# Sums over channels and heads: products of the full array in place of GpSimd sums and column tiles

## What is computed

```python
def layer(x, ...):
    h = rms_norm(x, norm_mix)
    p = h @ w_in
    y_a, ... = rwkv7_mix(p[..., :SHIFT_COLS], ...)      # 8 heads x 64
    y_b, ... = conv_mix(p[..., SHIFT_COLS:], ...)       # 512 channels
    x = x + concatenate([y_a, y_b], axis=-1) @ w_out
    x = x + moe_ffn(rms_norm(x, norm_ffn), ...)         # top 4 of 32 experts

# at the end of rwkv7_mix: a norm for each token and head, over 64 values
    mu = mean(y, axis=-1); var = mean(square(y - mu), axis=-1)
    y = ((y - mu) * rsqrt(var + GN_EPS)) * lnx_w + lnx_b
    y = (y + bonus) * g

# at the end of conv_mix: a norm for each token, over 512 channels
    mu = mean(z); var = mean(square(z - mu))
    z = (z - mu) * rsqrt(var + LN_EPS) * conv_ln_w + conv_ln_b
    z = z * sigmoid(z)
```

## Time and profile before

| | us |
|---|---|
| median of 3 runs | 1235.98 (1235.7 to 1237.92) |
| the profiled execution, own time | 1235.7 |
| its span | 1233.9 |
| TensorE busy | 1190.7 (96%) |
| VectorE busy | 452.6 (37%) |
| ScalarE busy | 194.5 (16%) |
| GpSimd busy | 73.0 (6%) |
| HBM read | 424.93 MB |

### The profile page before, as it was taken

How to read it: one execution, slowest core, us unless ns; L and a number is a source line. 1 busy time by engine, 2 the same in 40 slices (tenths; PEclk the granted TensorE clock), 3 DMA queues, 4 the chain that set the end, 5 groups by cost and what they waited for, 6 DMA issues and landing times.

```text
span 1233.9 us, 19174 instructions
## 1 busy us (share of the span) xinstructions
PE 1190.7 (96%) x8039; PEld 540.6 (44%) x8039; DVE 452.6 (37%) x987; ACT 194.5 (16%) x387; POOL 73.0 (6%) x113
## 2 busy tenths in 40 slices
PE   7999998999999999999999999999999999999995
PEld 5667798864333333333333333333333333333332
DVE  6657764243522333322222223323222222222324
ACT  3352223224100001101001000010000010000102
POOL 0303433030000000000000000000000000000000
PEclk9999999999999999999999999999999999999998
DMA  9421003188999999999999999999999999999994
GB/s 271 164 69 47 10 5 138 43 325 316 420 420 422 429 428 427 427 428 429 429 428 429 428 429 429 428 429 429 429 428 429 429 428 429 428 429 426 428 429 165
DMA packets 54637, 430.26 MB, mean 349 GB/s; under 512 B 13215, under 2 KB 26959, under 8 KB 29742
## 3 DMA queue, kind: packets, MB, share of 16 engines
q1 hardware_dynamic: 53146, 429.30, 84.1%
q10 hardware_dynamic: 1436, 0.16, 0.1%
HBM read 424.93 MB, written 4.48 MB: 348 GB/s over the span
## 4 chain that ended last, share of the span: by engine, by line
PE 59%; DMA 19%; DVE 1%; ACT 0%; issue 0%; DVEq 0%
PE bank L1793 40%; DMA ring<-in_w_up_dram 19%; PE bank L1771 6%; PE bank L1847 5%; PE bank L1778 2%; PE bank L1673 2%; PE bank L1722 1%; PE bank L1801 1%; PE bank L1819 1%; DVE arena L2138 0%; DVE arena L2132 0%; DVE arena L2078 0%; ACT ring L1619 0%; PE bank L1693 0%; PE bank L1842 0%
## 5 line engine op out<-in xcount | busy, mean ns | idle before, releaser
L1793 PE MATMUL bank<-ring,arena 128*64 128x512 f32 x1536 | 342.2, 594 | 7.2 <-DMA ring<-in_w_up_dram 6.5
L1793 PE MATMUL bank<-arena 128*64 128x512 f32 x1536 | 342.5, 593 | 6.4 <-DMA arena<-in_w_up_dram 6.4
L1793 PEld LDWEIGHTS bank<-ring,arena 128*64 128x64 f32 x1536 | 109.2, 137 | 218.5 <-issue 200.5
L1793 PEld LDWEIGHTS bank<-arena 128*64 128x64 f32 x1536 | 109.0, 136 | 217.2 <-issue 199.4
L2064 DVE TENSOR_SCALAR arena<-bank 128x512 f32<-128x512 f32 x32 | 22.1, 691 | 380.4 <-PE bank L1801 380.4
L2078 DVE TENSOR_TENSOR arena<-arena,bank 128x512 f32<-128x512 f32 x186 | 113.7, 679 | 1.6 <-PE bank L1847 1.6
L524 PE MATMUL bank<-arena,ring 128*128 128x336 f32 x352 | 103.6, 452 | 1.2 <-DVE arena L660 1.2
L1847 PE MATMUL bank<-arena 64*128 64x512 f32 (+1 forms) x384 | 91.1, 606 | 0.7 <-issue 0.7
L1771 PE MATMUL bank<-arena 128*64 128x512 f32 (+1 forms) x384 | 89.5, 600 | 0.1
L2068 DVE TENSOR_SCALAR arena<-bank 128x512 f32<-128x512 f32 x32 | 22.1, 691 | 176.4 <-PE bank L1801 176.4
L524 PEld LDWEIGHTS bank<-arena,ring 128*128 128x128 f32 x352 | 67.1, 192 | 34.8 <-issue 3.3
(11 more groups left out here) (356 smaller groups left out, 821.0 us busy)
## 6 DMA issues: line engine op xcount, KB each, us to landing
ring<-in_w_gate_dram SPq DMA_DIRECT2D x32, 2048.0 KB, 24.8
arena<-in_w_up_dram SPq DMA_DIRECT2D x32, 2048.0 KB, 27.9
ring<-in_w_down_dram SPq DMA_DIRECT2D x32, 2048.0 KB, 31.3
arena<-in_w_gate_dram SPq DMA_DIRECT2D x32, 2048.0 KB, 26.6
ring<-in_w_up_dram SPq DMA_DIRECT2D x32, 2048.0 KB, 29.1
arena<-in_w_down_dram SPq DMA_DIRECT2D x31, 2048.0 KB, 31.0
ring<-in_w_in_dram SPq DMA_DIRECT2D x11, 1024.0 KB, 5.8
ring<-in_w_out_dram SPq DMA_DIRECT2D x4, 1024.0 KB, 8.7
```

The lines of the kernel that those rows point to most:

```text
L1793: mm = M.matmul(bank[64 * hb:64 * hb + 64, b, :], tokens(cc), w[:, c, 512 * hb:512 * hb + 512], start=(cc == 0), stop=(w3 == 2 and cc == K ...
```

## The change

The constant `spread` and its five instructions go. In stage two GpSimd's four sums go; TensorE makes four products that add up in the bank, one for each tile, for the mean and for the variance. In stage three the mean is one product of the full array for each tile with `headones` (sum and spreading at once). The variance is summed onto 8 partitions, one for each head, with a new constant `headcol`, and spread again from these 8 with `headrow`; both are made at the head of stage three from two iotas of GpSimd and three instructions of VectorE. The sums of the variance stand behind d = 1 instead of 2, the rows behind d = 3 instead of 4, and ScalarE's squares stand ahead of its first `take_z`.

```diff
--- before.py
+++ after.py
@@ -117,7 +117,6 @@
         ident = take(P)
         ones = take(P)
         headones = take(P)
-        spread = take(P)
         identc = take(C)
         seqrow = take(NSEQ)
         rowf = take(1)
@@ -699,11 +698,6 @@
                 link(V.tensor_tensor(itmp, itmp, cgrp, ALU.is_equal))
                 V.tensor_tensor(cmask[:, 2, :], cmask[:, 2, :], itmp, ALU.mult)
                 link(V.tensor_tensor(cmask[:, 3, :], cmask[:, 3, :], itmp, ALU.mult))
-                V.tensor_scalar(cgrp, icol, 6, None, ALU.logical_shift_right)
-                link(V.tensor_scalar(itmp, irow, 4, None, ALU.logical_shift_right))
-                link(V.tensor_scalar(itmp, itmp, 1, None, ALU.bitwise_and))
-                link(V.tensor_tensor(itmp, itmp, cgrp, ALU.is_equal))
-                V.tensor_scalar(spread, itmp, 1.0 / 16, None, ALU.mult)
                 dve.wait_ge(R["vec_ready"], 1)
                 link(V.tensor_scalar(vecA[:, V_OMKA:V_OMKA + 4], vecA[:, V_KA:V_KA + 4], -1.0, 1.0,
                                      ALU.mult, ALU.add))
@@ -841,7 +835,7 @@
             return RKq[64 * i:64 * i + 64, :, j * NT + ts:j * NT + ts + n]
 
         names = ["conv_step", "v_turned", "vtok_ready", "hat_ready",
-                 "zmean_done", "z_paired", "z_summed", "z_centered", "z_squared", "zvar_done", "zvar_ready", "zroot_ready", "zinv_ready",
+                 "zmean_done", "z_centered", "z_squared", "zvar_done", "zvar_ready", "zroot_ready", "zinv_ready",
                  "z_normed", "z_affine", "z_sig", "zT_ready",
                  "kt_turned", "bt_turned", "ktok_ready", "btok_ready", "sk_done", "sb_done", "n_done",
                  "sk_read", "sb_read", "n_read", "a0_ready", "n_ready", "at0_ready",
@@ -912,15 +906,8 @@
                     pool.wait_ge(S["n_ready"], p + 1)
                     T.tensor_tensor(AT[p].rearrange("p q j c -> p (q j) c"), n8, b2(cneg0T, 8), ALU.mult)\
                         .then_inc(S["at0_ready"], 1)
+                pool.wait_ge(S["seq4_ready"], 1)
                 pool.wait_ge(S["conv_step"], CONV_LATE)
-                T.tensor_tensor(zsq[:, 0:2, :], zT[:, 0:2, :], zT[:, 2:4, :], ALU.add).then_inc(S["z_paired"], 1)
-                pool.wait_ge(S["z_paired"], 1)
-                T.tensor_tensor(zsq[:, 0, :], zsq[:, 0, :], zsq[:, 1, :], ALU.add).then_inc(S["z_summed"], 1)
-                pool.wait_ge(S["z_squared"], 4)
-                T.tensor_tensor(zsq[:, 0:2, :], zsq[:, 0:2, :], zsq[:, 2:4, :], ALU.add).then_inc(S["z_paired"], 1)
-                pool.wait_ge(S["z_paired"], 2)
-                T.tensor_tensor(zsq[:, 0, :], zsq[:, 0, :], zsq[:, 1, :], ALU.add).then_inc(S["z_summed"], 1)
-                pool.wait_ge(S["seq4_ready"], 1)
                 pool.wait_ge(S["ktok_ready"], 3)
                 pool.wait_ge(S["btok_ready"], 3)
                 s4 = seq4.unsqueeze(1).unsqueeze(3).broadcast_to([P, NPAIR, 4, HD])
@@ -1072,14 +1059,16 @@
                     for p in range(NP3):
                         level_a(l, p)
                     if l == 2:
+                        pe.wait_ge(S["conv_step"], CONV_LATE)
                         pe.wait_ge(S["at_ready"], number_t[(2, 2)] + 1)
-                        pe.wait_ge(S["z_summed"], 1)
-                        M.matmul(bank[:, 7, 0:NT], ones, zsq[:, 0, :], start=True, stop=True)\
-                            .then_inc(S["zmean_done"], 1)
+                        for j in range(4):
+                            mm = M.matmul(bank[:, 7, 0:NT], ones, zT[:, j, :], start=(j == 0), stop=(j == 3))
+                        mm.then_inc(S["zmean_done"], 1)
                     if l == 3:
-                        pe.wait_ge(S["z_summed"], 2)
-                        M.matmul(bank[:, 7, 0:NT], ones, zsq[:, 0, :], start=True, stop=True)\
-                            .then_inc(S["zvar_done"], 1)
+                        pe.wait_ge(S["z_squared"], 4)
+                        for j in range(4):
+                            mm = M.matmul(bank[:, 7, 0:NT], ones, zsq[:, j, :], start=(j == 0), stop=(j == 3))
+                        mm.then_inc(S["zvar_done"], 1)
 
                 level_g(4, 0)
                 level_g(4, 1)
@@ -1327,6 +1316,8 @@
         u1 = at_word(30336, 512)
         sg = at_word(30848, 512)
         sel3 = at_word(29824, 3 * NOVER, NE)
+        headrow = at_word(29824, 512)
+        headrow_i = at_word(30336, 512).bitcast(I32)
         lg4 = at_word(30336, NT)
         sq4 = at_word(30848, NT)
         ycg = at_word(31184, 4, NT)
@@ -1336,6 +1327,9 @@
         Pm = at_word(32528, 3, C)
         esel = at_word(32720, C, dt=BF16)
         rk = at_word(32752, 3)
+        headcol_i = at_word(32756, 4 * NH).bitcast(I32)
+        headcol = at_word(32788, 4, NH)
+        headtmp = at_word(32820, 4 * NH)
         over = [7424]
 
         def bit(*shape, dt=F32):
@@ -1361,7 +1355,8 @@
 
         F = {n: lsem("f_" + n) for n in [
             "x_in", "bias_raw", "wr_in", "gffn_in", "gfin_in", "bias_in",
-            "ysum_done", "ysum_ready", "ymean_done", "y_centered", "y_squared", "yvar_done", "yroot_ready", "yinv_ready", "ybc_done",
+            "headrow_made", "headcol_made", "heads_ready",
+            "ymean_done", "y_centered", "y_squared", "yvar_done", "yroot_ready", "yinv_ready", "ybc_done",
             "yT_ready", "dstep",
             "zp_done", "zp_ready", "zx_ready", "xy_done", "x2_ready", "xsq_ready", "ssq_done", "lg_done", "lg4_ready", "sq4_ready",
             "acc_turned", "acc_ready", "ms_ready", "rms_ready", "wrg_ready", "ssum_done", "logits_done",
@@ -1502,6 +1497,11 @@
             def _(pool):
                 T = nc.gpsimd
 
+                T.iota(headrow_i[0:NH, :].rearrange("p (h k) -> p h k", k=HD), [[1, NH], [0, HD]], base=0,
+                       channel_multiplier=-1).then_inc(F["headrow_made"], 1)
+                T.iota(headcol_i.rearrange("p (j h) -> p j h", h=NH), [[-P, 4], [HD, NH]], base=0,
+                       channel_multiplier=-1).then_inc(F["headcol_made"], 1)
+
                 pool.wait_ge(F["x_in"], 16)
                 for d in range(KC):
                     pool.wait_ge(F["zp_ready"], d + 1)
@@ -1520,24 +1520,21 @@
                 A = nc.scalar
                 act.wait_ge(F["zp_turned"], 1)
                 A.copy(zpT, bank[:, 3, 0:NPAIR * HD].rearrange("p (j k) -> p j k", j=NPAIR)).then_inc(F["zp_copied"], 1)
-                act.wait_ge(F["ysum_done"], 1)
-                A.copy(yrstd, bank[:, 4, 0:NT]).then_inc(F["ysum_ready"], 1)
+                for j in range(4):
+                    act.wait_ge(F["y_centered"], j + 1)
+                    A.activation(ysq[:, j, :], yT[:, j, :], ACT.Square).then_inc(F["y_squared"], 1)
 
                 def take_z(d):
                     act.wait_ge(F["zp_done"], d + 1)
                     A.copy(x2T[:, d, :], bank[:, d % 2, 0:NT]).then_inc(F["zp_ready"], 1)
 
                 take_z(0)
-                for j in range(4):
-                    act.wait_ge(F["y_centered"], j + 1)
-                    A.activation(ysq[:, j, :], yT[:, j, :], ACT.Square).then_inc(F["y_squared"], 1)
                 take_z(1)
-                take_z(2)
                 act.wait_ge(F["yvar_done"], 1)
-                act.wait_ge(F["eps_set"], 1)
-                A.activation(yrstd, bank[:, 2, 0:NT], ACT.Sqrt, bias=eps, scale=1.0 / HD)\
+                act.wait_ge(F["heads_ready"], 1)
+                A.activation(yrstd[0:NH, :], bank[0:NH, 2, 0:NT], ACT.Sqrt, bias=eps[0:NH, :], scale=1.0 / HD)\
                     .then_inc(F["yroot_ready"], 1)
-                for d in range(3, KC):
+                for d in range(2, KC):
                     take_z(d)
 
                 def take_acc(hb, i):
@@ -1647,21 +1644,9 @@
                         mm = M.matmul(bank[64 * i:64 * i + 64, 3, HD * j:HD * j + HD], Zc[64 * i:64 * i + 64, j, :],
                                       ident[64 * i:64 * i + 64, 64 * i:64 * i + 64], start=True, stop=True)
                 mm.then_inc(F["zp_turned"], 1)
-
-                def head_sums(b, v):
-
-                    for j in range(4):
-                        mm = M.matmul(bank[32 * j:32 * j + 32, b, 0:NT], headones[:, 48:80], v[:, j, :],
-                                      start=True, stop=True)
-                    return mm
-
-                def head_rows(v, done):
-
-                    for j in range(4):
-                        M.matmul(bank[:, 4 + j, 0:NT], spread[32 * j:32 * j + 32, :], v[32 * j:32 * j + 32, :],
-                                 start=True, stop=True).then_inc(F[done], 1)
-
-                head_sums(4, yT).then_inc(F["ysum_done"], 1)
+                for j in range(4):
+                    M.matmul(bank[:, 4 + j, 0:NT], headones, yT[:, j, :], start=True, stop=True)\
+                        .then_inc(F["ymean_done"], 1)
                 for d in range(KC):
                     o = bank[:, d % 2, 0:NT]
                     if d == 0:
@@ -1675,15 +1660,18 @@
```

(28 more changed lines are left out.)

## The result

The changed kernel takes 1244.8 us (median of 4 runs, 1244.21 to 1245.92) against 1236.95 (4 runs, 1235.7 to 1238.28) for the kernel before on the same chip: ratio 1.0064, 95% interval 1.0047 to 1.0082. It is slower, as forecast, by more than forecast. Its profiled execution took 1242.7 us for a span of 1240.9, so 7.0 more than before.

A forecast was written before the change was run, and what follows sets the result against it. The weight stream sets the last 900 us, but its steady start waits for TensorE. Terms 0 + 0 + 1.70 + 4.23 = +5.93 gave a median of 1241.9 us, 0.48% slower; range 1238.4 to 1244.8.

The forecast's parts named there:

- rival B: Stage two: the stall moves along with the program, so the mean's +1.38 stays; +7.3 in all, 1243.3 us; chance 0.15.
- Stage one, 0: Stage one: dropping five VectorE instructions only lengthens VectorE's idle time of 6.84 us; term 0.
- Mean, 0: Stage two's mean: products end 1.38 us later, but TensorE's 2.38 us stall shrinks to 1.0 and absorbs it; term 0.
- Variance, +1.70: Stage two's variance: no wait goes, three more products of 0.567 us come, no new wait; +1.70 us.
- Stage three, +4.23: Stage three's per-head sums: blocks of 2.27, 2.46 and 2.46 us replace 2.96 us in all; +4.23, ends +0.9 and +6.9.
- the expected absence of waits: Stage three: no new TensorE wait was expected to show; the reciprocal would be ready with 1.6 us of slack.
- Clock kept: Stage three's head: the low-clock stretch, costing 1.9 us, stays as before; a stretch more or less is 1.9 either way.
- Passing through to the end: Ninth weight load: whatever delays TensorE before it, at 307.57 us, makes the end later by the same amount.

The follow-up runs named there:

- e2: Kernel before with the change's stage-three part (and stage one's) alone: 1242.14 us, ratio 1.0026 to the kernel before.
- e4: Kernel after with the four loads of w_out spread over stage two: 1244.45 us, ratio 1.0056 to the kernel before.
- e10: Kernel after with two of the four loads of w_out moved to the head of stage three: 1241.46 us, ratio 1.0026 to the kernel before.
- e9: Kernel before with two of the four loads of w_out moved to the head of stage three: 1234.53 us, ratio 0.9970.
- e7: Kernel before with all four loads of w_out issued 3.5 us later, behind the mean's product: 1239.01 us, one run.
- e6: Kernel before with only stage two's variance over channels made as four products: 1238.65 us, one run.
- e8: Kernel before with four more products, results unused, in stage three: 1238.43 us, against 1240.47 for the kernel before beside it, one run each.
- e11: Kernel before with eight extra products ahead of stage two's mean: 1237.18 us, against 1237.02 for the kernel before, one run each.
- e1: Kernel before with the change's stage-two part alone, mean and variance as four products each: 1241.86 us, ratio 1.0025.
- e12: Kernel before with sixteen extra products ahead of stage two's mean: 1242.52 us, against 1237.02 for the kernel before, one run each.

## Why the prediction was wrong

Slower was right, and rival B, the forecast's nearest neighbour, is the case that came: +7.0 between the profiles, where B said +7.3. What the steps measured:

- **Stage one, 0.** Right as far as it can be seen: stage two begins between 145.23 and 146.31 in the four profiles that hold this edit (after, e2, e4, e10), and between 145.07 and 147.31 in the ten that don't. An effect of some tenths could hide in this spread.
- **Mean, 0, "the stall should end at the same time and TensorE waits 1.0 instead of 2.38".** This step failed. The size of the delay was right (level three starts 1.46 us later behind level two's end, +1.38 put; without a stall, e9 against e10, 1.38), and the wait ahead of the product became 0.24 shorter, 0.3 put. But the stall kept its length (2.51), and the 1.5 passed through. I took the end of a burst and the end of a stall that lay 0.6 us apart for cause and effect; after, they lie 2 us apart, in e7 the stall ends inside the burst. The loads made the block late, which was the right half of the step; what ends the stall is the block's own packet, 2.5 us after its start in both kernels, and TensorE's delay of 1.5 us moved that packet too: it starts 8.1 us behind level two's end before and 9.6 after. In e7 it starts 7.9 us behind, with the loads 3.5 us later.
- **Variance, +1.70.** Right: +1.69 by the stretch behind it (49.96 against 48.27), and 2.54 after against 0.83 before for the block itself. By the net stretch e6 has 97.27 - 95.37 = +1.9, within what that correction is worth. No new wait.
- **Stage three, +4.23.** Right: 64.70 - 60.71 = +4.0. The narrow products cost 2.43 and 2.52, where 2.46 was taken from the earlier trace rows, not 0.78 and not 3.81; the expected absence of waits is there (slack of the reciprocal 1.75, put at 1.6).
- **Clock kept.** Right in number, and that is in part luck: two low stretches before (147 to 150.5, 246 to 249.5) and two after (205 to 208.3, 249.3 to 252.7), but stage two's at another place; other profiles have from one to four. The size was put a little high: 3.8 us at a mean of 0.55 lose 3.8 x 0.45 = 1.7 us, not 1.9.
- **Passing through to the end.** Right: 926.33 and 926.20; e8.

The steps add to +1.46 + 1.69 + 3.99 = 7.1 against 5.93; the profiles are 7.0 apart. The forecast of 1241.9 missed 1244.8 by 2.9: 1.2 is the mean's step, 1.0 is the median of the kernel before, 1236.95 here and not 1235.98, and the remaining 0.7 lies within the interval, since the ratio 1.0064 (+7.9, interval +5.8 to +10.1) holds 7.1.

## What to carry to other kernels

The stall that TensorE's row calls "issue" stood here at a count of instructions in the program. Do not let such a stall take up a delay in a sum merely because it overlaps a burst of loads: look at how many instructions lie ahead of it and when the packet of the instruction queue starts, and move the loads instead, here for 0.3%. Array packing of small products is worth what the rows say: four products of 32 columns or rows side by side took 0.70 to 0.78 us, four narrow ones one after the other 2.4 to 2.5, as much as full ones, and where TensorE bounds the way to a weight stream, as here, such products are not paid for by relieving VectorE or GpSimd, which were waiting. And when an effect is half a per cent, compare stretches between fixed points of two traces; single times of this kernel differ by as much.

## What was not expected of the hardware

- The clock's low level comes at other places in executions of the same code in stage two: 147 to 150.5 before and 195 to 198.5 in e8, whose stage two is the same, and 199 to 206 in e9, none in e11. A stretch is 3.4 or 6.8 us long. What one costs can be read from the way to level two's end: 39.79 to 39.80 us in the three profiles with a stretch of 3.4 us there, 38.30 to 38.32 in ten of the others, so 1.5 us. From the start of stage two to the ninth load the profiles have between one such length (e11) and five (e1); that this makes a good part of the spread of the kernel before, 1234.65 to 1241.85, is an estimate.
- The reciprocal of 8 partitions took 2.24 us, that of 128 took 2.25.
- VectorE's pass over 1344 columns took 2.14 us beside GpSimd's sums before, and 1.55 after, where GpSimd had nothing left to do:

```profile
190.22 1.55 DVE L1256 TENSOR_TENSOR arena<-arena 128x1344 f32<-128x1344 f32 x1
```

GpSimd's own sum of 336 columns took 2.09 beside it and 0.89 alone. The DMA engines are not the reason: in e12 the same two took 2.13 and 2.10 with the loads long through. In e6 the pass meets GpSimd's last expansion (189.64 to 193.33) and takes three times as long:

```profile
190.17 4.58 DVE L1264 TENSOR_TENSOR arena<-arena 128x1344 f32<-128x1344 f32 x1
```

It ends 1.42 us after GpSimd's instruction does. In the kernel before it also ends 1.42 us after GpSimd's first sum (191.27 to 192.69), and GpSimd's second sum ends 0.75 us after the pass. The rows look like turns, one engine standing until the other is done. In the kernel before and after nobody waited for either.
